# Reordering the beginning of a one-layer decoder step on one core

## The reference, cut to what matters

```
mod = silu(c) @ w_ada + b_ada                       # 9 vectors of 1024: sh1, sc1, ga1, sh2, ...
x = x + 0.5*ga1 * swiglu(rms(x, g1)*(1+sc1) + sh1)  # first FFN: 1024 -> 2 x 2816 -> 1024
x = x + ga2 * mixer(rms(x, g2)*(1+sc2) + sh2)       # RG-LRU and mLSTM branches
x = x + 0.5*ga3 * swiglu(rms(x, g3)*(1+sc3) + sh3)  # second FFN
y = rms(x, g_final)
rms(x, g) = x * rsqrt(mean(x*x) + 1e-6) * g
```

## Time and profile before

| | us |
|---|---|
| median of 3 timed runs | 1497.8 (1496.0 to 1500.41) |
| the profiled execution, time | 1491.6 |
| its span | 1489.8 |
| PE busy in the span | 1425.9 (96%) |
| DVE, ACT, POOL busy | 713.6, 548.5, 53.4 |
| mean granted clock of PE | 0.984 of full |

### The profile page before, as it was taken

The page is one execution under the profiler, slowest core; times in us unless marked ns, Lnnn a source line. Parts: engine busy times, 40 slices in busy tenths (PEclk is TensorE's granted clock), DMA queues, the critical chain, the costliest instruction groups (busy, mean ns, idle before and its releaser), DMA issues.

```text
span 1489.8 us, 29260 instructions
## 1 busy us (share of the span) xinstructions
PE 1425.9 (96%) x11964; PEld 1389.4 (93%) x11964; DVE 713.6 (48%) x1203; ACT 548.5 (37%) x769; POOL 53.4 (4%) x114
## 2 busy tenths in 40 slices
PE   5799999999999898999999999999989999999996
PEld 4699999999999798999999989999989999999996
DVE  4454444545333556666374756744553333333333
ACT  3343344434222456733434335422243332322221
POOL 1000000000000100000011112200000000000000
PEclk9999999999999899999999999999989999999998
DMA  9255555455333321233244535423322323223231
GB/s 370 73 165 163 166 165 170 157 155 166 102 92 92 117 84 59 86 103 90 82 123 135 154 100 163 131 94 96 89 69 85 98 84 98 85 83 92 90 88 57
DMA packets 49586, 173.99 MB, mean 117 GB/s; under 512 B 6608, under 2 KB 6672, under 8 KB 49136
## 3 DMA queue, kind: packets, MB, share of 16 engines
q1 hardware_dynamic: 43200, 151.68, 32.8%
q0 software_dynamic: 6032, 19.25, 4.0%
q10 hardware_dynamic: 288, 2.13, 0.4%
HBM read 161.28 MB, written 11.75 MB: 116 GB/s over the span
## 4 chain that ended last, share of the span: by engine, by line
PE 90%; DVE 6%; ACT 2%; issue 1%; DMA 0%; DVEq 0%; ACTq 0%
PE big L523 79%; PE bank L541 2%; PE bank L774 2%; PE bank L766 1%; PE big L626 1%; DVE w_l L1169 1%; PE bank L780 1%; PE bank L734 1%; DVE xn_l L1237 1%; DVE tb L1216 1%; PE bank L798 1%; DVE ssq L1183 0%; ACT tb L855 0%; PE bank L753 0%; ACT w_h L841 0%
## 5 line engine op out<-in xcount | busy, mean ns | idle before, releaser
L1169 DVE TENSOR_TENSOR w_l<-raw,w_h 128x1024 fp32r<-128x1024 f32 (+2 forms) x272 | 321.5, 1187 | 369.1 <-ACT w_h L842 365.1
L523 PE MATMUL big<-xn_h,w_h 128*128 128x260 f32 x2288 | 468.2, 286 | 10.2 <-DVE xn_l L1237 7.4
L523 PE MATMUL big<-xn_h,w_l 128*128 128x260 f32 x2288 | 461.9, 283 | 0.0
L523 PE MATMUL big<-xn_l,w_h 128*128 128x260 f32 x2288 | 461.0, 283 | 0.0
L523 PEld LDWEIGHTS big<-xn_h,w_h 128*128 128x128 f32 x2288 | 355.2, 189 | 15.0 <-issue 10.2
L842 ACT ACTIVATE w_h<-raw 128x1024 fp32r<-128x1024 f32 (+2 forms) x272 | 276.3, 1020 | 244.1 <-PE big L523 241.4
L523 PEld LDWEIGHTS big<-xn_l,w_h 128*128 128x128 f32 x2288 | 353.9, 189 | 0.0
L523 PEld LDWEIGHTS big<-xn_h,w_l 128*128 128x128 f32 x2288 | 353.6, 189 | 0.0
L523 PE MATMUL big<-hid_h,w_h 128*128 128x260 f32 x704 | 142.2, 283 | 0.0
L523 PE MATMUL big<-hid_h,w_l 128*128 128x260 f32 x704 | 141.5, 282 | 0.0
L523 PE MATMUL big<-hid_l,w_h 128*128 128x260 f32 x704 | 141.5, 282 | 0.0
(11 more groups left out here) (291 smaller groups left out, 1336.2 us busy)
## 6 DMA issues: line engine op xcount, KB each, us to landing
raw<-ff_in SPq DMA_DIRECT2D x88, 512.0 KB, 3.6
raw<-w_mix SPq DMA_DIRECT2D x81, 512.0 KB, 3.6
raw<-w_ada SPq DMA_DIRECT2D x55, 512.0 KB, 3.7
raw<-ff_out SPq DMA_DIRECT2D x32, 512.0 KB, 3.5
adaw<-w_ada SPq DMA_DIRECT2D x17, 512.0 KB, 14.0
cst_c<-st_C POOLq DMA_DIRECT2D x32, 256.0 KB, 4.3
o_Cs<-cst_c POOLq DMA_DIRECT2D x32, 256.0 KB, 3.4
raw<-ff_out SPq DMA_DIRECT2D x16, 384.0 KB, 3.1
```

Of the source, the lines that this page charges most:

```text
L523: ins = nc.tensor.matmul(out[:, hf, 0:HALF], a[:, w], b[:, k0 + i, hf * HALF:(hf + 1) * HALF], start=first and i == 0 and s == 0, stop=las ...
L1169: V.tensor_tensor(w_l[c % RING][:, from_:width], raw[:, c % RING, from_:width], w_h[c % RING][:, from_:width], ALU.subtract).then_inc(w_lo ...
```

## The change

Five edits, all in the beginning:

- Squares alternate between `tb[2]` and `tb[3]`; a square waits for the add of the one before the last.
- ACT runs a root of one element right after the squares, so that the root's table is loaded there; the wait for the constants moves with it.
- PE: condition product 0 moves ahead of the spread.
- PE: the rows and the condition product of group g + 1 move ahead of the tile products of group g.
- ACT splits chunk 2 between `first_take(3)` and `first_high(3)`, DVE after `first_norm(3)`; step 0 of the first turn leaves it out on both.

```diff
@@ PE
             first_sums()
             for c in range(4, 6):
                 first_rows(c)
+            first_back(0)
             first_spread()
-            first_back(0)
             for c in range(6, 10):
                 first_rows(c)
             first_back(1)
-            first_products(0)
             for c in range(10, 12):
                 first_rows(c)
-            first_products(1)
+            first_products(0)
+            first_back(2)
             for c in range(12, 14):
                 first_rows(c)
-            first_back(2)
+            first_products(1)
             for c in range(14, 16):
                 first_rows(c)
-            first_products(2)
             first_back(3)
             first_rows(16)
+            first_products(2)
+            first_back(4)
             first_products(3)
-            first_back(4)
             ffn(C_FFI1, T_FFI1, UP1, UP1_LOOPS, S_XN1, S_HID1)
@@ ACT, a step of ffn
-                    split(c + LEAD, after + (c + LEAD),
-                          i * (16 * len(pattern) // RING) + arrivals(c + LEAD), urgent=k == URGENT and "M" in pattern)
+                    if not (isinstance(i, int) and k == 0):
+                        split(c + LEAD, after + (c + LEAD), i * (16 * len(pattern) // RING) + arrivals(c + LEAD),
+                              urgent=k == URGENT and "M" in pattern)
@@ ACT, squares
-                squares(kt, kt)
+                if kt >= 2:
+                    act.wait_ge(ssq_ready, kt - 1)
+                A(tb[2 + kt % 2][:, :], x[:, kt, :], ACT.Square).then_inc(sq_ready, 1)
+            act.wait_ge(const_ready, 7)
+            A(warm[:, :], eps_t[0:1, :], ACT.Sqrt)
@@ ACT, the beginning
             first_take(0)
-            act.wait_ge(const_ready, 7)
             act.wait_ge(job_done, 1)
...
             first_take(3)
+            split(C_FFI1 + 2, C_FFI1 + 2, arrivals(C_FFI1 + 2))
             first_high(3)
@@ DVE, a step of ffn
-                    split(c + LEAD, after + (c + LEAD), urgent=i + 1 if k == URGENT and "M" in pattern else None)
+                    if not (isinstance(i, int) and k == 0):
+                        split(c + LEAD, after + (c + LEAD), urgent=i + 1 if k == URGENT and "M" in pattern else None)
@@ DVE, squares
-                add_squares(kt, kt == 0)
+                dve.wait_ge(sq_ready, kt + 1)
+                if kt == 0:
+                    V.tensor_copy(ssq[:, :], tb[2][:, :]).then_inc(ssq_ready, 1)
+                else:
+                    dve.wait_ge(ssq_ready, kt)
+                    V.tensor_tensor(ssq[:, :], ssq[:, :], tb[2 + kt % 2][:, :], ALU.add).then_inc(ssq_ready, 1)
@@ DVE, the beginning
             first_norm(3)
+            split(C_FFI1 + 2, C_FFI1 + 2)
             first_mods(4)
```

## The result

| | before | after |
|---|---|---|
| median of the timed runs | 1497.99 (1496.0 to 1500.41) | 1481.43 (1480.13 to 1483.38) |
| the profiled execution: time, span | 1491.6, 1489.8 | 1481.4, 1479.6 |
| mean granted clock of PE | 0.984 | 0.984 |
| start of chunk 4 | 65.60 | 51.75 |

The ratio is 0.989 (95% interval 0.9874 to 0.9906): 16.6 us faster, where 10.8 were forecast, and outside the range of 1483 to 1494.5. The direction was right; the size was not. The two profiles alone would have hidden this: their spans differ by 10.2. So there are two things to explain, the 13.85 at chunk 4 instead of 10.8, and the timed 16.6 beside the profiled 10.2.

What follows compares the result with a forecast made beforehand. PE bounds the kernel (busy 96% of the span), so an earlier chunk 4 carries to the end. 1.85 + 4.6 (order) + 1.6 (split) + 4.1 (clock) = 12.2, less 1.4, gives 10.8: 1487.0, range 1483 to 1494.5.

Steps and rivals of the forecast that it cites:

- front, up to products 0: Sums, spread and first norm up to products 0: earlier sums and condition product 0 ahead of the spread gain 1.85.
- order of the groups: Four groups on PE: each group's norm is hidden behind the products before it, gaining 4.6.
- early split: Between products 3 and chunk 4: chunk 2 split earlier, so chunk 4 starts 3.5 after the products, not 5.1; gain 1.6.
- half clock, less the fall left in: Groups' products on PE: three slow groups return to full clock, gaining 4.1, less 1.4 for one fall remaining.
- my figure: Start of the first norm product, forecast at 23.4 instead of 25.24.
- Rows 10 and 11: Moved in front of products 0: covered by the splits with 1.1 to spare; without that cover they cost 1.1.
- The waits for the take: PE before condition products 2 and 3: new waits for the take of rows, 1.4 and 0.6.
- The wait before rows 8: PE idle ahead of rows 8: 3.47 before, followed by full pace; 2.2 in the new order.
- The rule of the Trainium skill: PE clock: activity releases the throttled state, so no fall in the new order; 12.2 gained. Full-clock rival, chance 0.29.
- Against its own time: Whole kernel: the profiled execution's 10.8 subtracted from the timed median of 1497.8, 6.2 above the profiled 1491.6, giving 1487.0.

Runs made afterwards that it cites:

- before_again: The kernel before, unchanged, timed and profiled a second time: 1497.92 against 1497.87, ratio 1.0001; chunk 4 at 67.93.
- fill_before: Kernel before, same order, with matmuls whose results nobody reads put on PE in its early waits: 1490.03, ratio 0.9947.
- order_fill: Kernel before with only PE's order of groups changed, plus 24 and 8 unread matmuls before rows 8 and condition product 2: 1483.92, ratio 0.9913.
- late_table: Kernel after without the early root of one element, so the root's table loads where it did before: 1480.88, profiled execution only.
- late_split: Kernel after with the third chunk split in step 0 of the first turn again: 1481.7, profiled execution only; chunk 4 at 53.32.
- old_order: Kernel after with the old order of the groups on PE, other edits kept: 1492.27, ratio 0.9957.

## Why the prediction was wrong, point by point

The terms of the forecast, beside what the runs give for them. The measured column goes from before_again to the changed kernel, by way of fill_before and order_fill (rounded).

| ahead of chunk 4 | forecast | measured |
|---|---|---|
| front, up to products 0 | 1.85 | 3.0 |
| order of the groups | 4.6 | 6.5 |
| early split | 1.6 | 0.5 |
| half clock, less the fall left in | 4.1 - 1.4 | 6.3 |
| sum | 10.8 | 16.2 |

**Front of the chain: right in mechanism.** The sums moved up to the end of chunk 3's rows, and DMA sets that end. Undoing the double buffer made the sums 1.06 later (forecast 0.77), undoing the swap cost 1.3 from the sums on (1.1), the table 0 (0). That chunk 4 moved by just 0.76 and 1.03 in these two runs is partly luck, as said there. The rest of the 3.0, about 0.7, is PE's pace in the early stage, that is the execution. The same holds for the lead of 0.9 that the norm product had over my figure: chunk 3 landed 0.26 earlier, and the spread took 1.48 and not 2.08.

**Rows 10 and 11: right, and closer to the edge than forecast.** They are covered by the splits, but chunk 11 was waited for by 0.49, and three of the other kernels waited 0.55 to 4.0 for a chunk (late_table, late_split, old_order). A front that moves up further would meet the DMA.

**Order of the groups: right mechanism, 6.5 instead of 4.6.** The waits for the take appeared where they were forecast (1.33 and 0.72 before condition products 2 and 3). From products 0 to the end of products 3 the order gained 5.2 (24.0 in fill_before, 18.9 in order_fill), near the 4.6. The other 1.3 was booked in the wrong place: with condition product 4 ahead of products 3, the last modulation tile and the first split run beside the products in any case. I had put that under the early split (1.6), which measured 0.5. Together they are 6.9 against my 6.2.

**The clock: the step that failed.** The mechanism was right, the size was not: I took off 2.7 net, and it measured 6.3, which is the largest part of the miss. Three things were wrong in it. The groups' loss of 4.1 was read from one execution in which the clock fell less than usual; from products 0 to chunk 4 before_again took 33.98 and fill_before 29.01, a loss of 5.0. The wait before rows 8 was priced at nothing, because the earlier trace rows shows full pace behind it; in before_again those rows ran at half pace (1.94, not 1.08), and products 0 started 1.3 later than in fill_before. And I let one fall stay in the new order, because its longest wait was as long as the shortest that had preceded a fall; one profile of the changed kernel shows none, the other one, worth 1.1. The rule of the Trainium skill that I weighed (TensorE: Matmul & The Clock Gate, "What's actually happening": activity releases the throttled state) gave 12.2, nearer than my forecast, though one of the two profiles of the changed kernel has a fall all the same. The same section of the Trainium skill says that the watching does not restart with the kernel; one kernel with chunk 4 at 65.6 and at 67.9 is in keeping with that, but no run here shows it to be the reason.

**Against its own time: wrong for a part of the 6.2.** I subtracted the 10.8, worked out on an execution of 1491.6, from the median of 1497.8, and let the 6.2 between them stand as if it belonged to both kernels. For what lies behind chunk 4 that was right: the first profile lost 4.4 less there than before_again, and the changed kernel has the usual loss. But 2.3 of it was half clock in the very stretch that the change rebuilds, and belonged to the gain. Profiles of usual executions close the sum: 67.93 - 51.75 = 16.2 ahead of chunk 4 and 1428.6 - 1427.9 = 0.7 behind it are 16.9, beside the timed 16.6. With the second profile of the changed kernel (chunk 4 at 52.85) it is 15.8, between the two timed gains of 16.6 and 13.8. The two first profiles instead show 13.85 gained ahead and 3.7 given back behind, 10.2; that would have looked like a confirmation of 10.8.

What stays open: what decides in which execution the clock falls, and where. The traces show that it falls behind PE's waits and that filling them stops most of it, not why the same waits led to groups of 4.65 and 4.35 in one execution and to two of 5.54 in the other. Open too is what sets PE's pace in the first 20 us.

## What to carry to other kernels

When the profiled execution is faster than all timed runs of the same kernel, find out by which term before pricing a change with it: here the gap was the clock, and a third of it sat in the stretch under study. A better order that keeps PE going pays twice, once for the wait and once for the clock behind it; here the order alone was worth 6.5 at full clock and 11.4 at chunk 4 with the clock. Plain filling leaves the wait and pays for the clock alone (6.3). And ask of two edits at one place which of them is left over when the other is made: the early split was mostly paid for by the new order.

## What the runs showed of the hardware

Matmuls whose results nobody reads made the kernel before 7.8 faster (1490.03 against 1497.87) and the kernel after 3.6 faster (1478.5 against 1482.09); the granted clock behind the filled waits was 1.00 in the beginning, and 0.83 to 1.00 and not 0.66 around the later norms. The clock column of the profile shows 1.00 in the first 20 us also where PE runs at half pace: 32 products of rows took 1.93 at 18.04 and 1.08 at 25.78 in the same profile, both under 1.00, so early durations have to be read themselves. That pace differs between executions: the ten matmuls of the first sums took 2.29 or 2.30 in twelve of the fourteen profiles and 1.27 or 1.28 in the other two (late_split, old_order).
